# Half of the v rows added by TensorE, gathers in the order c, x, c, and a timetable for the woven work

## What is computed

```python
def peer_ffn(h, wq, subkeys, u, v):
    ...
    s1, i1 = lax.top_k(scores[..., 0, :], PEER_TOPK)      # 16 of 128
    s2, i2 = lax.top_k(scores[..., 1, :], PEER_TOPK)
    ...
    top, pos = lax.top_k(cand, PEER_TOPK)                 # 16 of 256, 8 heads
    eidx = jnp.take_along_axis(cidx, pos, axis=-1)        # 128 experts a token
    gate = jax.nn.softmax(top, axis=-1).astype(h.dtype)
    ...
        act = jax.nn.gelu(jnp.einsum('ted,td->te', u[ek], hk), approximate=False)
        return jnp.einsum('te,ted->td', gk * act, v[ek])
```

## Time and profile before

| | us |
|---|---|
| median of three runs | 4341.35 |
| lowest, highest | 4330.94, 4344.67 |
| the profiled execution | 4339.68, span 4337.8 |
| busy: PE, PE weight load, DVE, ACT, POOL | 1973, 1354, 3195, 709, 935 |
| mean granted TensorE clock | 0.723 of full speed |

### The profile page before, as it was taken

One profiled execution on the slowest core, in us unless ns is written; L12 is line 12 of the kernel. 1 busy time (PEld: TensorE's weight loads), 2 busy tenths in 40 slices (PEclk: granted clock), 3 DMA queues, 4 the chain that ended last, 5 costly groups with the idle time before them and its releaser, 6 DMA issues.

```text
span 4337.8 us, 29160 instructions
## 1 busy us (share of the span) xinstructions
PE 1973.4 (45%) x9362; PEld 1353.8 (31%) x9362; DVE 3194.8 (74%) x5528; ACT 708.9 (16%) x1125; POOL 934.8 (22%) x803
## 2 busy tenths in 40 slices
PE   7787111208754121110418642121230476977688
PEld 1676000006633000000318530000110344947386
DVE  0464899998976999999886569999878753546354
ACT  0312000001110000001112110000100242523053
POOL 0000333332222333333320013333334100000000
PEclk9898555658877555555759876555565687978789
DMA  7324899998887899999963269898999512533054
GB/s 262 136 83 154 343 362 351 354 382 331 323 321 275 346 365 368 360 367 358 373 248 122 104 235 376 354 360 337 358 365 363 209 68 94 188 126 132 14 189 146
DMA packets 275597, 1150.09 MB, mean 265 GB/s; under 512 B 19466, under 2 KB 19573, under 8 KB 176720
## 3 DMA queue, kind: packets, MB, share of 16 engines
q0 software_dynamic: 113264, 814.26, 47.7%
q1 hardware_dynamic: 162016, 334.19, 21.3%
q10 hardware_dynamic: 192, 0.20, 0.0%
HBM read 1147.33 MB, written 1.25 MB: 265 GB/s over the span
## 4 chain that ended last, share of the span: by engine, by line
DVE 42%; PE 27%; DMA 18%; issue 10%; ACT 2%; SPq 0%; POOL 0%; POOLq 0%; DVEq 0%; ACTq 0%
DVE arena L1631 15%; DMA arena<-in_peer_uv,arena 13%; DVE arena L1609 8%; PE ps L631 5%; PE ps L633 5%; PE ps L632 5%; PE ps L616 4%; DVE w_lo L1297 2%; DMA vec<-mods 1%; PE ps L705 1%; DVE arena L1403 1%; DVE arena L1526 1%; DVE arena L1529 1%; DVE arena L1535 1%; PE ps L625 1%
## 5 line engine op out<-in xcount | busy, mean ns | idle before, releaser
L1897 POOL DMA_INDIRECT arena<-in_peer_uv,arena x768 | 916.2, 1193 | 2321.3 <-DVE arena L1631 1547.2
L1631 DVE SCALAR_TENSOR_TENSOR arena<-arena 128x1024 f32<-128x1024 f32 x762 | 977.8, 1283 | 13.6
L705 PE MATMUL ps<-ring,condS 128*2 128x512 f32 x768 | 400.6, 684 | 1266.7 <-DVE mod_io L1673 1239.5
L1609 DVE CUSTOM_DVE_ANT_0 arena<-arena,hA 128x1024 f32<-128x1024 f32 x512 | 625.1, 1221 | 91.3 <-DMA arena<-in_peer_uv,arena 86.7
L705 PEld LDWEIGHTS ps<-ring,condS 128*2 128x2 f32 x768 | 67.7, 92 | 1596.3 <-DVE mod_io L1673 1278.3
L1297 DVE TENSOR_TENSOR w_lo<-ring,w_hi 128x1024 fp32r<-128x1024 f32 x272 | 326.1, 1223 | 216.6 <-ACT w_hi L996 209.9
L1120 ACT ACTIVATE arena<-arena 128x2 f32<-128x2 f32 x384 | 78.1, 203 | 2259.4 <-DVE arena L1609 2259.2
L631 PE MATMUL ps<-hT_hi,w_hi 128*128 128x256 f32 x1408 | 407.8, 290 | 44.1 <-DVE hT_lo L1305 38.3
L632 PE MATMUL ps<-hT_lo,w_hi 128*128 128x256 f32 x1408 | 404.8, 287 | 0.0
L633 PE MATMUL ps<-hT_hi,w_lo 128*128 128x256 f32 x1408 | 404.4, 287 | 0.0
L1609 DVE CUSTOM_DVE_ANT_0 arena<-arena,hB 128x1024 f32<-128x1024 f32 x256 | 312.6, 1221 | 46.5 <-DMA arena<-in_peer_uv,arena 43.9
(11 more groups left out here) (266 smaller groups left out, 2955.0 us busy)
## 6 DMA issues: line engine op xcount, KB each, us to landing
ring<-in_w_mod SPq DMA_DIRECT2D x48, 2048.0 KB
ring<-in_w_in SPq DMA_DIRECT2D x64, 512.0 KB, 6.4
ring<-in_w_mlp_in SPq DMA_DIRECT2D x64, 512.0 KB, 5.9
ring<-in_w_mlp_out SPq DMA_DIRECT2D x64, 512.0 KB, 5.6
ring<-in_w_in SPq DMA_DIRECT2D x11, 2048.0 KB
ring<-in_peer_wq SPq DMA_DIRECT2D x32, 512.0 KB, 7.9
vec<-mods SPq DMA_DIRECT2D x31, 512.0 KB, 7.7
ring<-in_w_out SPq DMA_DIRECT2D x6, 2048.0 KB
```

The source lines that it names most:

```text
L705: mm = pe.matmul(o, condS[:, k, 2 * (l // 2):2 * (l // 2) + 2], ring[:, s, k, :], start=k == 0, stop=k == KT - 1)
L1609: dve.tensor_tensor_reduce(row, row, peer_buf[p][:, t, :], 1.0, 0.0, ALU.mult, ALU.add, dots[:, col:col + 1]).then_inc(dot_done, 1)
L1631: ins = dve.scalar_tensor_tensor(acc, row, c, acc, ALU.mult, ALU.add)
L1897: pool.indirect_dma_start(uv[:, j % SLOTS, :], None, A["peer_uv"], at).then_inc(uv_full[j % SLOTS], 16)
```

## The change

**Rows.** Of each two selections the second, and all of the first 24, is added by PE. DVE writes the diagonal matrix `ident * coef * gate` over the used u row, and PE multiplies it with the v row in two products of 512 columns into PSUM banks 6 and 7, which collect a segment's sum. DVE adds only the other rows. A slot is released by PE (`pe_added`) or DVE (`dve_added`). At the end of a segment DVE adds the PSUM sum to `acc`.

**Order.** The gathers go through seven segments: context tile 0 (128), the first 32 of context tile 1, both latent tiles of layer 0 (256), the last 96 of the context, then layer 1. So the latents of layer 1 can start while the context's last 96 are gathered.

**Timetable.** `weave(first, last, segment, *streams)` runs on PE too. Each piece carries the number of the pair of selections behind which it runs, and the streams go in a fixed order. The latent mixers are `front_pieces` with half a level in each of 16 pairs; PE's banks 4 and 5 serve the levels. A choice has five pairs (three for the first four). A first score tile is stored in DRAM (`held`) and loaded again.

**Moved.** Layer 1's latent norm, projections (no longer split) and levels go under the context's last 96 selections; what follows without gathers has the context's norm, its three projections (now split), the scan, then the latents' output. The filters go behind the modulations, under the gathers of pairs 136 to 154, and their spectra through DRAM. Of the first modulation eight chunks come first, with the context norm beside chunks 4 to 8, two in the context's mixer, two under the gathers. Three small tables are loaded first, and the masks come as bytes. The state products of the context mixer come behind its output projection.

```diff
+        SEGS = [(0, 0, 0, NSEL), (0, 1, 0, NQ), (1, 0, 0, NSEL), (1, 1, 0, NSEL), (0, 1, NQ, NSEL),
+                (2, 0, 0, NSEL), (2, 1, 0, NSEL)]
...
+        def on_pe(j):
+            return j % 2 == 1 or j < 24
...
+        for j, k in enumerate([(0, 0, 1), (0, 0, 2), (0, 0, 3), (0, 1, 0)]):
+            PICK_SLOTS[k] = [3 * j, 3 * j, 3 * j + 1, 3 * j + 1, 3 * j + 2]
+        for j, k in enumerate(PICK_ORDER[5:13]):
+            PICK_SLOTS[k] = [61 + 5 * j + i for i in range(5)]
+        for j, k in enumerate(PICK_ORDER[13:16]):
+            PICK_SLOTS[k] = [104 + 5 * j + i for i in range(5)]
+        for j, k in enumerate(PICK_ORDER[17:]):
+            PICK_SLOTS[k] = [FIRST_PAIRS + 5 * j + i for i in range(5)]
...
+            def __init__(self, norm, base, gap):
...
+                r = base + 4 + gap
+                self.chunk = [[base, base, base + 1, base + 1], [base + 2, base + 2, base + 3, base + 3],
+                              [r, r, r + 1, r + 1], [r + 1, r + 2, r + 2, r + 3]]
+                self.chunk += [[r + 4 * c + b for b in range(1, 5)] for c in range(4)]
...
+                self.level = [r + 4 + i for i in range(16)]
+                self.tail = r + 20
...
+        TIMES = {1: Times(2, 7, 2), 3: Times(PAIRS[3], PAIRS[3] + 5, 0)}
+        OUT, POST, WQ, SCORES = 38, 43, 48, 60
+        MOD_AT = {1: 84, 2: 108, 3: FIRST_PAIRS + 36}
+        FILTERS = 136
+        KV = FIRST_PAIRS + 66
...
+        def weave(first, last, segment, *streams):
+            due = [next(x, None) for x in streams]
+            for g in range(first, last + 1):
+                segment(g, first, last)
+                for n, x in enumerate(streams):
+                    while due[n] is not None and due[n] <= g:
+                        due[n] = next(x, None)
...
+            modulation0(0, 6)
+            modulated0(4)
+            load_rows("n_c0")
+            modulation0(6, 8)
+            weights(L_in[0])
+            modulation0(8, 10)
...
+            def level_pieces(m):
+                times, base = TIMES[m], {1: 9, 3: 25}[m]
+                for i in range(16):
+                    yield times.level[i]
+                    pe.wait_ge(lev_ready, base + i + 1)
...
+            def add_row(j):
...
+                pe.wait_ge(diag_ready, pe_upto[j + 1])
+                if start and seg:
+                    pe.wait_ge(sums_taken, seg)
+                for c in range(2):
+                    mm = pe.matmul(ps[:, 6 + c, :], uv[:, j % SLOTS, 0:P], uv[:, j % SLOTS, D + c * CW:D + (c + 1) * CW],
+                                   start=start, stop=stop)
+                mm.then_inc(pe_added, 1)
...
+            def segment(g, first, last):
+                if g > first:
+                    for j in (2 * g - 2, 2 * g - 1):
+                        if on_pe(j):
+                            add_row(j)
...
+            weave(0, FIRST_PAIRS, segment,
+                  itertools.chain(early_mods(), turn_norm_pieces("n_x0", TIMES[1].turn), front_pieces(1)), level_pieces(1),
+                  itertools.chain(back_pieces(1), turn_norm_pieces("p_x0", POST + 3), query_pieces(1), score_pieces(1),
+                                  modulation(1), modulation(2), filters(),
+                                  turn_norm_pieces("n_x1", TIMES[3].turn), front_pieces(3)), level_pieces(3))
...
+            def front_pieces(m):
...
+                for i in range(16):
+                    yield times.level[i]
...
+                        lev, d = (i - 1) // 2, (i - 1) % 2
+                        dve.wait_ge(lev_mm, base + i + 1)
+                        st.do(put_level(d, lev, 0, 4))
+                        ins = put_level(d, lev, 1, 5)
+                        if d == 0:
+                            ins.then_inc(lev_ready, 1)
+                        else:
+                            st.do(ins)
+                            scan_update(lev, True, lambda ins: ins.then_inc(lev_ready, 1))
...
+            def weigh(j):
...
+                dve.wait_ge(gelu_done, j // 2 + 1)
+                if on_pe(j):
+                    dve.tensor_scalar(uv[:, j % SLOTS, 0:P], ident[:, :], c, gate, ALU.mult, ALU.mult).then_inc(diag_ready, 1)
+                else:
+                    dve.tensor_tensor(c, c, gate, ALU.mult).then_inc(coef_ready, 1)
...
+            def segment(g, first, last):
...
+                done = (2 * g - 2, 2 * g - 1) if g > first else ()
+                for s in range(2):
+                    if g < last:
+                        dot(2 * g + s)
+                    if s == 0:
+                        for j in done:
+                            weigh(j)
+                    if done and not on_pe(done[s]):
+                        add_row(done[s])
...
+                k = j - SLOTS
+                if k >= 0 and on_pe(k):
+                    pool.wait_ge(pe_added, pe_upto[k + 1])
+                elif k >= 0:
+                    pool.wait_ge(dve_added, dve_upto[k + 1])
```

More of the change, by code:

```diff
@@ new lines, in turn_norm_pieces, with modulation0 @@
+            def turn_norm_pieces(name, slot):
+                yield from turn_pieces(name, norm_buf[name], normed, lambda t: NT * norm_no[name] + t + 1, slot)
+            def modulation0(lo, hi):
+                for L, c in L_mod0[lo:hi]:
+                    s = enter(L, 0, 0, L.e0)
+                    for k in range(KT):
+                        mm = pe.matmul(ps[0:2, 2 * (L.e0 % 2), :], condS[:, k, 0:2], ring[:, s, k, :],
+                                       start=k == 0, stop=k == KT - 1)
+                    mm.then_inc(ring_done, 1)
@@ L804, in mixer @@
[L804 to L806 removed]
+                for c in range(3, 8):
+                    part(c, 0, 2)
+                    level(2 * (c - 3))
+                    part(c, 2, 4)
+                    if c < 7:
+                        level(2 * (c - 3) + 1)
+                modulation0(8, 9)
+                pe.wait_ge(scan_ready, 1)
+                attend(0, range(HEADS)).then_inc(o_done, 1)
+                mean_square(0, 6)
@@ new lines, in mixer0, with front_pieces @@
+            def mixer0():
+                L = L_in[0]
+                for c in range(2):
+                    forget(L, c)
+                for c in range(2, 8):
+                    take_chunk(L, c)
+                modulation0(8, 9)
+                square_out(0)
+                root_out(0, 6)
+                modulation0(9, 10)
+                take_states(0)
+            def front_pieces(m):
+                L, times = L_in[m], TIMES[m]
+                yield times.evict[0]
+                if m == 1:
+                    act.wait_ge(held_out, 16)
+                    act.wait_ge(picks, pick_no[0, 1, 0] + 1)
+                else:
+                    act.wait_ge(spec_out, 32)
+                for c in range(8):
+                    yield times.evict[c]
+                    if c < 2:
+                        forget(L, c)
+                    else:
+                        take_chunk(L, c)
@@ L1190, in _, with early_mods @@
-            run(norm_pieces("n_x1"), mixer(3), norm_pieces("p_x1"), peer_queries(2), peer_part(2, 0))
-            weave(2, RATE[2], segment, blend(peer_parts(2), modulation(3)), norm_pieces("n_kv"), kv_pieces())
+            def early_mods():
+                for c in range(10, 12):
+                    yield c - 8
+                    modulation0(c, c + 1)
+            modulation0(0, 4)
+            root(0)
+            modulation0(4, 6)
+            split_high(L_in[0], 0)
+            modulation0(6, 8)
@@ new lines, in _ @@
+            root(0)
+            turn_parts("n_c1")
+            L = L_in[2]
+            forget(L, 0)
+            forget(L, 1)
+            copy_tokens(L, 2, ivN1)
+            take_states(1)
+            square_out(2)
+            root_out(2, 6)
+            turn_norm("p_x1")
+            queries(2)
+            take_score(2, 0)
+            pick_exp((2, 0, 0))
+            take_score(2, 1)
+            weave(FIRST_PAIRS, ALL_PAIRS, segment, gate_piece(3, FIRST_PAIRS), pick_pieces(PICK_ORDER[17:]), modulation(3),
+                  norm_pieces("n_kv", KV), kv_pieces())
@@ L1685, in _, with segment @@
-            run(norm_pieces("n_x1", xs), mixer(3), norm_pieces("p_x1", xs), peer_queries(2), peer_part(2, 0))
+                    dve.tensor_tensor(acc, sums, pgate[:, :], ALU.mult).then_inc(sums_taken, 1)
+                    dve.wait_ge(sums_taken, seg + 1)
+                dst = peer_dst[p][:, t, :]
+                dve.tensor_tensor(dst, dst, acc, ALU.add).then_inc(peer_out, 1)
+                dve.wait_ge(peer_out, seg + 1)
+            def segment(g, first, last):
+                done = (2 * g - 2, 2 * g - 1) if g > first else ()
+                for s in range(2):
+                    if g < last:
+                        dot(2 * g + s)
[4 more added lines that the diff above has]
+                        add_row(done[s])
+                if done and 2 * g in SEG_END:
+                    flush(SEG_END.index(2 * g))
```

(14 more changed lines are left out.)

1260 lines of the change are left out of this document (752 added, 508 removed).

## The result

The changed kernel takes **4417.11 us** (median of 4 executions, 4408.73 to 4430.6) beside 4341.7 of the kernel before on the same chip: ratio 1.0181, 95% interval 1.0146 to 1.0216. It is slower, since the interval leaves out no change, but whether by more or less than 2% the interval leaves open. That is the side that was forecast, 46 us above the predicted 4371: inside the range of 4210 to 4470, and 1 us beyond the 4416 that the forecast gave as its own error. The profiled execution has a span of 4408.0 us, 70.2 more than before.

The account below looks back on a forecast made before the run. DVE was taken to set the pace where other work is woven between the pairs, the transfers elsewhere. The terms 199 + 13 - 57 - 69 - 55 = +31 gave 4371 us, range 4210 to 4470.

Parts of the forecast that it names:

- level slots: Slots (one pair of selections plus woven pieces) 17 to 32 and 221 to 236, half a level each: 200 us per region.
- first two passes: Gathers before the stretch without gathers, slots 0 to 255: 2002 us forecast against 1803, +199.
- stretch without gathers: Between second and third pass, 319 us before: context norm, projections, scans and attention, forecast 69 us shorter.
- third pass: Last gathers, from slot 256: 35 slots with choices 259 us, the rest 589; 848 against 835, +13.
- lock-step: Level slots: DVE waits for TensorE's half level, queued behind a row waiting for DVE's diagonal; 4 to 5 us a slot.
- Slots 12 to 17 and 213 to 221: TensorE's chunk quarters up to each level region's first slot: 57 us for 12 to 16, 82 for 213 to 220.
- The first rival: Level slots: the wait is not paid, each region costs 117 us; whole 4205 us, chance 0.18.
- The clock rival: TensorE stays at half clock, 1.2 GHz, level slots included: about +100 us, whole 4471 us; chance 0.15.
- Choice slots: Slots with pieces of a choice of experts, such as 61 to 100 and 256 to 290: DVE sets 7.4 us each.
- Slots bound by transfers: Where gathers set the pace, such as slots 154 to 212: 5.4 us a slot, 323 us for these 59.
- The second rival: Transfers go faster when DVE lets them, 415 GB/s: 252 transfer-bound slots gain 70 us, whole 4301 us; chance 0.12.
- the rival built on it: Diagonal products in DVE's two-port mode hold up POOL's issue of gathers: +37 us, whole 4408 us; chance 0.07.

## Why the prediction came out as it did

The side was right, and the mechanism of the level slots. Step by step, in the profiled executions, against the kernel before. Here a stretch with gathers runs, in both kernels, from the issue of its first gather to the end of its last row sum. The prediction had taken 2236, 2555 and 3390 as marks in the kernel before; counted this way they are 2243.7, 2551.0 and 3394.1:

| step | predicted | measured |
|---|---|---|
| front, to the first gather | -57 | -53 (433.6 to 380.6) |
| first two passes | +199 | +246 (1810 to 2056) |
| stretch without gathers | -69 | -80 (307 to 227) |
| third pass | +13 | +17 (843 to 860) |
| from there to the end, filters | -55 | -60 (944 to 884) |
| sum | +31 | +70 |

- **Level slots.** The mechanism is shown twice, by moving the half level and by taking the row away. The regions took 229 and 230 us instead of 200, but only 12 of these 29 us belong to the lock-step: slots 18 to 32 took 197 us, 185 predicted (with the 6 us added for a cold TensorE). In 18 to 29 it was 13.7 us a slot instead of 12.5, since the row on TensorE, taken at 1.9 us, took 3.4 on average (ten of the twelve 3.4 to 3.8, which is half clock or near it, behind a wait); half a level and the chunk took 6.1 instead of 5.3. I had the bound "up to twice that at half clock" in the price of a slot and didn't carry it into the sum. DVE's waits for the half levels were forecast at 60 us a region and measured at 90.
- **Slots 12 to 17 and 213 to 221.** The other 17 us of each region are its first slot, 32 us where I had 15. Slots 12 to 16 took 40 us instead of 57 and 213 to 220 58 instead of 82, since DVE doesn't wait for the chunk quarters there (its idle time in 12 to 16 is 14 us, all for gathers); TensorE is late with them and DVE pays in slot 17, 22.4 us. Taken together, 12 to 17 took 71.7 us (72 predicted) and 213 to 221 took 91 (97). The work was priced nearly right and put in the wrong slots.
- **The first rival** (the wait is not paid) was wrong for this order: in the first region only two of sixteen slots, both without a projection chunk, were under 11 us (9.5 and 10.9). Its 117 us of DVE work are the floor that the kernel with the half level first comes near, at 135; the 17 us between them are the wait of the first slot.
- **The clock rival** named 4471. Over whole stretches the clock went up, as I had argued (0.69 and 0.58 to 0.79; third pass 0.59 to 0.74), and its low clock in the level slots went with the lock-step and left with it. But there a part of that rival came true: the rows at 3.4 to 3.8 us in most level slots are rows at half clock, inside a lock-step that the forecast had priced without them.
- **Choice slots.** 7.4 us forecast; 7.7 measured in 61 to 100, 7.2 in 256 to 290. That choices in a row leave the transfers idle (0.75 forecast, 0.79 measured in the third pass) is shown by spreading them, which gave 24 us.
- **Slots bound by transfers.** 5.76 us a slot in 154 to 212 against 5.47 forecast. This is partly a misreading: I counted 66 or 67 gathers in the 180 us of the earlier trace rows, but the row has 32 instructions of ACT, one for two gathers, so 64, and 5.6 us a pair. The changed kernel took 5.59 in the middle of the stretch (slots 160 to 205), so the rate there had not changed, and 11 of the 17 us are this price. The other error is one of reasoning. I read "0.97 busy" as a resource at its limit. The second rival was nearer the mark: the transfers do go faster, 402 GB/s, but in these runs only with both rows on TensorE and both diagonals early. A lighter DVE by itself (one row in two on TensorE: 340 us, none: 339) brought nothing, as forecast, and a lighter one still (both rows on TensorE) was slower, 368 us.
- **Diagonal products and POOL.** A gather takes POOL 1177 ns on average with 396 diagonals about, 1193 ns in the kernel before. The Trainium skill, "SBUF — State Buffer", section "SBUF: two separate sides", lets VectorE in a two-port mode lock GpSimd out while it writes descriptors; in this trace it can't be seen, and the rival built on it fell: without a single diagonal slots 154 to 212 took 338.6 us, with them 339.7. Of the ceiling of 435 GB/s for the ports in the Trainium skill, "DMA: Bandwidth & Descriptors", section "Where 436 GB/s comes from", the best 280 us reached 402. The same section says that for transfers between the memory and SBUF the memory side binds, at about 358; here, on one core, 375 and 402 GB/s were measured, so the measurement decides.
- **Stretch without gathers.** The output projection begins 99 us after the last row sum (2436.9 to 2535.8); before it was 180, and I had 109 on this count. The rest is as long as before, 128 us and 127. Why the 99 are 10 us less than forecast was not looked into.
- **Filters.** 60 us against 55, with the scatter of the last 880 us in it.

The sum missed by 39 us in the profiled executions: 47 in the first two passes, less 8 in the other steps together. Of the 47, the level slots 18 to 32 and 222 to 236 are 24 and slots 154 to 212 are 17; the other regions miss by 0 to 8 us with either sign, which comes to 6.

## What to carry to other kernels

When an engine in a woven schedule gets a small piece of another engine's work, put the pieces in the order of who waits: what the other engine waits for goes first, what depends on that engine's newest result goes next, and bulk work last. Here that order alone decided between 1.8% slower and 2.5% faster. A DMA share of 0.98 doesn't prove that the transfers are the limit: look who ends the idle time of the engine that issues them, and follow the ring of buffers, since a release that stands behind the next transfer's wait can cost rate (368 us against 320 here). Rows on TensorE beside its own chunks cost time in three stretches here and gained in the level slots once the order was right, so decide it by stretch. And work that an engine is handed faster than it does it is paid later, by whoever waits for that engine next: here in the first level slot.

## What the runs showed of the hardware

TensorE's granted clock differed with the order of the work alone, and with it the waits of a few us. For the same 620 records of a region it was 0.83, with 159 us busy, where it waited up to 6.7 us in each slot; 0.93 and 136 us with the half level ahead of the chunk; 0.99 and 127 us with the half level first of all. Two fp32 products of 128x512 took 3.78 us at a granted clock of 0.50, which is 1.2 GHz (607.5 to 611.3 us of the changed kernel), and 1.88 at 1.00, which is 2.4 (605.8 to 607.6 with the half level first). The 16 DMA engines read 0.98 busy at 375 GB/s and 1.00 at 402 with the same gathers, so the share told little of what was left.
